# Latent attention: content and rotary rows of a head in one tile of 96 rows, one score product a head

## What is computed

```python
qc = (rmsnorm(cq, g_q) @ w_uq).reshape(B, T, C_HEADS, C_NOPE + C_ROPE)     # 4 heads, 64 + 32
q_nope, q_pe = qc[..., :C_NOPE], rope(qc[..., C_NOPE:], pos)
q_lat = jnp.einsum('bthn,hrn->bthr', q_nope, w_uk)
ckv = rmsnorm(ckv_raw, g_kv)
kpe = rope(kpe_raw[:, :, None, :], pos)[:, :, 0, :]                          # one for all heads
# mla_attend, for blocks of 128 queries over all keys before them:
s = (jnp.einsum('...qhr,...kr->...hqk', q_lat, ckv)
     + jnp.einsum('...qhp,...kp->...hqk', q_pe, kpe)) * ((C_NOPE + C_ROPE) ** -0.5)
p = jax.nn.softmax(s, axis=-1)
```

## Time and profile before

| | |
|---|---|
| Runs | 2032.88, 2032.96, 2033.73 us |
| Profiled execution | 2033.12 us; its span in the trace is 2031.3 us |
| TensorE busy | 2013.7 us, 99% of the span |
| VectorE, ScalarE, GpSimd busy | 82%, 48%, 18% |
| Share of TensorE in the chain that ended last | 94% |
| Mixing, layer 0 and layer 1 | about 405 to 619 us and 1401 to 1617 us |

### The profile page before, as it was taken

The page is one execution under the profiler, slowest core; times in us unless marked ns, Lnnn a source line. Parts: engine busy times, 40 slices in busy tenths (PEclk is TensorE's granted clock), DMA queues, the critical chain, the costliest instruction groups (busy, mean ns, idle before and its releaser), DMA issues.

```text
span 2031.3 us, 40732 instructions
## 1 busy us (share of the span) xinstructions
PE 2013.7 (99%) x15315; PEld 1961.2 (97%) x15315; DVE 1665.6 (82%) x2456; ACT 972.5 (48%) x1768; POOL 356.6 (18%) x218
## 2 busy tenths in 40 slices
PE   8999999999999999999999999999999999999998
PEld 7999999999889999999999999999987899999998
DVE  7999998755667999998689999976466599999975
ACT  6544453354546544453364444534546474444532
POOL 1222200042112222200012221002321213222000
PEclk8999999999999999999999999999999999999999
DMA  4323223342122232332222322324221123322321
GB/s 135 104 83 103 91 85 95 83 106 67 35 55 84 87 100 89 97 93 79 79 91 96 103 83 89 106 79 114 81 62 45 61 65 104 96 89 80 107 87 66
DMA packets 234855, 175.40 MB, mean 86 GB/s; under 512 B 35185, under 2 KB 231025, under 8 KB 234737
## 3 DMA queue, kind: packets, MB, share of 16 engines
q1 hardware_dynamic: 232624, 171.68, 28.3%
q10 hardware_dynamic: 2112, 2.10, 0.3%
HBM read 170.14 MB, written 3.62 MB: 86 GB/s over the span
## 4 chain that ended last, share of the span: by engine, by line
PE 94%; DVE 3%; ACT 2%; issue 1%; DMA 1%; ACTq 0%; DVEq 0%; SPq 0%
PE pair L1474 43%; PE pair L1423 32%; PE pair L1597 9%; PE pair L1530 2%; PE pair L1744 1%; PE pair L1724 1%; DVE t_parts L2067 1%; PE pair L1735 1%; PE pair L1730 1%; PE pair L1767 1%; PE pair L1752 1%; DMA x_tok<-in_x_prompt_dram 0%; ACT square L928 0%; PE pair L1760 0%; DVE t_parts L2350 0%
## 5 line engine op out<-in xcount | busy, mean ns | idle before, releaser
L1474 PE MATMUL pair<-t_parts,chunk_high 128*128 128x288 f32 x4480 | 893.5, 296 | 1.6 <-issue 1.2
L1474 PEld LDWEIGHTS pair<-t_parts,chunk_high 128*128 128x128 f32 x4480 | 719.5, 189 | 2.7 <-DVE chunk_low L2032 2.7
L1474 PE MATMUL pair<-t_parts,chunk_low 128*128 128x288 f32 x2240 | 661.6, 295 | 0.0
L1474 PEld LDWEIGHTS pair<-t_parts,chunk_low 128*128 128x128 f32 x2240 | 421.5, 188 | 0.0
L973 ACT ACTIVATE chunk_high<-chunk_sum 128x512 fp32r<-128x512 f32 x320 | 199.4, 631 | 380.4 <-DVE chunk_sum L2020 184.7
L870 POOL TENSOR_TENSOR chunk_low<-set_raw,chunk_high 128x512 fp32r<-128x512 f32 x160 | 229.4, 1443 | 716.4 <-ACT chunk_high L973 716.4
L864 POOL TENSOR_TENSOR w_low<-raw,w_high 128x1024 fp32r<-128x1024 f32 (+1 forms) x46 | 114.0, 2482 | 589.4 <-ACT w_high L921 589.4
L2032 DVE TENSOR_TENSOR chunk_low<-chunk_sum,chunk_high 128x512 fp32r<-128x512 f32 x320 | 207.1, 689 | 8.1 <-ACT chunk_high L973 0.5
L1423 PE MATMUL pair<-hidden_high,w_high 128*128 128x288 f32 x896 | 192.2, 296 | 0.0
L1423 PE MATMUL pair<-hidden_high,w_low 128*128 128x288 f32 x896 | 191.9, 296 | 0.0
L1423 PE MATMUL pair<-hidden_low,w_high 128*128 128x288 f32 x896 | 191.7, 296 | 0.0
(11 more groups left out here) (297 smaller groups left out, 3785.5 us busy)
## 6 DMA issues: line engine op xcount, KB each, us to landing
set_raw<-in_w_up_dram SPq DMA_DIRECT2D x44, 1024.0 KB, 5.4
set_raw<-in_w_gate_dram SPq DMA_DIRECT2D x44, 1024.0 KB, 5.4
raw<-in_w_down_dram SPq DMA_DIRECT2D x64, 448.0 KB, 3.6
down_raw<-in_w_down_dram SPq DMA_DIRECT2D x16, 1024.0 KB, 5.1
raw<-in_w_in_dram SPq DMA_DIRECT2D x20, 512.0 KB, 3.9
raw<-in_w_in_dram SPq DMA_DIRECT2D x16, 256.0 KB, 3.9
raw<-in_w_out_dram SPq DMA_DIRECT2D x8, 512.0 KB, 3.4
raw<-in_w_out_dram SPq DMA_DIRECT2D x16, 256.0 KB, 3.8
```

Source lines behind the costliest of these rows:

```text
L1474: mm = nc.tensor.matmul(out, c[:, j, p, :], tr[p // 2][:, seat(p), x, t, :], start=p == 0 and n == 0, stop=p == KP - 1 and n == 2)
```

## The change

Content and rotary rows of a head come to lie under each other in one tile of 96 rows: `keysT{h}` (64 content rows, 32 rotary rows, 832 keys) and `queriesT{h}` (576 columns), one pair of tiles a head. An MS unit is then one product of 96 rows a head, two a head in the sample unit (over the cache and over the new keys). The new keys stand ahead of the cache in the 832 columns.

To fill these tiles:

- `kn`: two ScalarE copies of 64 rows in place of one of 128, and behind those of `kn:0` three more that bring the rotated key to the heads 1 to 3 (32 rows, 576 columns, behind a wait on `rot:kpe.2`).
- `A:1` gets four ScalarE copies, in the list ahead of `T:8`: the rotated queries of each head to its tile (32 rows, 576 columns, behind a wait on `rot:qp.2`).
- `rot:kpe` gets four ScalarE copies, ahead of `E:9`: the cache's rotary key to each head (32 rows, 256 columns).
- `qn`: two VectorE copies of 64 rows in place of one of 128.
- `rot:qp` and `rot:kpe` multiply by the cosine in place, and so VectorE waits for TensorE's product by `rot32` ahead of its first instruction in place of its second.
- `tkpe` transposes from rows 64 to 95. `rot32` and `kpe_tok` lie elsewhere; the DMA of `rot32` is issued where it was.
- MS now waits for the last of the ScalarE copies of `kn:0`; the pair of `kn` is freed by its second copy.

```diff
@@ -215,9 +215,13 @@
     n = {"z": 0, "sumx": 1, "sumkv": 2, "sumq": 4, "tw": 1, "tv": 2, "tc": 2, "tk": 2, "tva": 2,
-         "rkv": 2, "tkpe": 2, "sw": 4, "rep": 1, "a": 1, "kn": 1, "E": 5, "O": 1, "ME": 2, "MO": 1, "ex": 1}.get(kind, 0)
+         "rkv": 2, "tkpe": 2, "sw": 4, "rep": 1, "a": 1, "kn": 2, "E": 5, "O": 1, "ME": 2, "MO": 1, "ex": 1}.get(kind, 0)
...
         n = 1 + arg
+    if step == "kn:0":
+        n = 2 + C_HEADS - 1
+    if step in ("A:1", "rot:kpe"):
+        n = C_HEADS
@@ -232,7 +236,7 @@
     kind, arg = split(step)
-    n = {"z": 1, "sumx": 2, "sumq": 3, "tckv": 2, "tw": 1, "rot": 3, "a": 4, "qp": 1, "qn": 1,
+    n = {"z": 1, "sumx": 2, "sumq": 3, "tckv": 2, "tw": 1, "rot": 3, "a": 4, "qp": 1, "qn": 2,
@@ -294,8 +298,12 @@
         return [("vector", f"rot:{arg}.0")]
-    if kind in ("z", "qp", "qn", "O", "MO", "A", "B"):
+    if kind in ("z", "qp", "O", "MO", "A", "B"):
         return [("vector", f"{step}.0")]
+    if kind == "qn":
+        return [("vector", f"{step}.1")]
+    if kind == "kn":
+        return [("scalar", f"{step}.1")]
@@ -335,7 +343,7 @@
         "S": lambda: ["tc.1"] if swa_unit(arg)[0] == 4 else [],
-        "MS": lambda: [f"kn:{mla_unit(arg)[1]}.0", "tc.1"],
+        "MS": lambda: [scalar_ops(s)[-1] for s in ("kn:0", "kn:1", "A:1", "rot:kpe")],
@@ -355,7 +363,7 @@
         "S": lambda: ["rot:k.2"] + [f"rot:q{2 * swa_unit(arg)[1] + e}.2" for e in range(2)],
-        "MS": lambda: ["rot:qp.2", "rot:kpe.2", f"qn:{mla_unit(arg)[1]}.0"],
+        "MS": lambda: ["rot:kpe.2", f"qn:{mla_unit(arg)[1]}.1"],
@@ -518,17 +526,16 @@
         KEYS = PAST + NT
-        knT = [mix(f"k_nopeT{j}", [P, KEYS]) for j in range(2)]
-        qnT = [mix(f"q_nopeT{j}", [P, NT]) for j in range(2)]
-        qpT = mix("q_peT", [P, NT])
-        kpeT = mix("kpeT", [P, NT])
+        kS = [mix(f"keysT{j}", [P, KEYS]) for j in range(C_HEADS)]
+        qS = [mix(f"queriesT{j}", [P, NT]) for j in range(C_HEADS)]
         kpe_rep = mix("kpe_rep", [P, NT])
-        rot32 = mix("rot32", [P, P])
...
         vc_tok = mix("vc_tok", [P, 7, C_HEADS * C_V])
-        kpe_tok = mix("kpe_tok", [P, 5, C_ROPE])
         assert cursor[0] <= temp0
+        rot32 = at("rot32", [P, P], F32, temp0 + U)
+        kpe_tok = at("kpe_tok", [P, 5, C_ROPE], F32, temp0 + U + P * 4)
+        NOPE, ROPE, BOTH = slice(0, C_NOPE), slice(C_NOPE, C_NOPE + C_ROPE), slice(0, C_NOPE + C_ROPE)
@@ -1265,6 +1272,15 @@
                         continue
+                    if step == "A:1":
+                        dve_did(act, layer, "rot:qp.2")
+                        for h_ in range(C_HEADS):
+                            copy(qS[h_][ROPE], zs[1][32 * h_:32 * h_ + 32], f"{step}.{h_}")
+                        continue
+                    if step == "rot:kpe":
+                        for h_ in range(C_HEADS):
+                            copy(kS[h_][ROPE, NT:KEYS], ckpeT[ROPE], f"{step}.{h_}")
+                        continue
@@ -1341,7 +1357,12 @@
                     elif kind == "kn":
-                        copy(knT[arg][:, :], flat(p)[:, 0:KEYS], f"{step}.0")
+                        for j in range(2):
+                            copy(kS[2 * arg + j][NOPE], flat(p)[64 * j:64 * j + 64, 0:KEYS], f"{step}.{j}")
+                        if arg == 0:
+                            dve_did(act, layer, "rot:kpe.2")
+                            for h_ in range(1, C_HEADS):
+                                copy(kS[h_][ROPE, 0:NT], kS[0][ROPE, 0:NT], f"{step}.{1 + h_}")
@@ -1688,11 +1709,12 @@
                         rows = C_ROPE if kind == "tkpe" else P
-                        src = {"tv": vT, "tckv": ckvT, "tkpe": kpeT, "tva": zs[1 - arg] if kind == "tva" else None}[kind]
+                        part = ROPE if kind == "tkpe" else slice(0, P)
+                        src = {"tv": vT, "tckv": ckvT, "tkpe": kS[0], "tva": zs[1 - arg] if kind == "tva" else None}[kind]
...
                             dst = ps[p][0:n, 0, t * rows:(t + 1) * rows] if t < 4 else ps[p][0:n, 1, 0:rows]
-                            mm = nc.tensor.transpose(dst, src[0:rows, t0:t0 + n], ident[0:rows, 0:rows])
+                            mm = nc.tensor.transpose(dst, src[part, t0:t0 + n], ident[part, part])
@@ -1711,7 +1733,7 @@
                         up = wuk[:, 2 * arg:2 * arg + 2, :].rearrange("p h n -> p (h n)")
-                        for col, keys, n in ((0, ckvT[:, 0:SEQ], SEQ), (SEQ, cT[:, P:3 * P], PAST), (SEQ + PAST, ckvT[:, SEQ:NT], DEC)):
+                        for col, keys, n in ((0, ckvT[:, 0:SEQ], SEQ), (SEQ, ckvT[:, SEQ:NT], DEC), (NT, cT[:, P:3 * P], PAST)):
@@ -1726,14 +1748,9 @@
                         for j in range(2):
-                            r = slice(64 * j, 64 * j + 64)
-                            nc.tensor.matmul(ps[p][0:nq, j, 0:W], qnT[pair][r, t0:t0 + nq], knT[pair][r, SEQ:KEYS] if i == 4 else knT[pair][r, 0:W],
-                                             start=True, stop=False)
-                        for k_pe, at0, col, n in ((ckpeT, 0, 0, PAST), (kpeT, SEQ, PAST, DEC)) if i == 4 else ((kpeT, 0, 0, W),):
-                            for j in range(2):
-                                r = slice(32 * (2 * pair + j), 32 * (2 * pair + j) + 32)
-                                mm = nc.tensor.matmul(ps[p][0:nq, j, col:col + n], qpT[r, t0:t0 + nq], k_pe[r, at0:at0 + n],
-                                                      start=False, stop=col + n == W)
+                            h_ = 2 * pair + j
+                            for col, at0, n in ((0, NT, PAST), (PAST, SEQ, DEC)) if i == 4 else ((0, 0, W),):
+                                mm = nc.tensor.matmul(ps[p][0:nq, j, col:col + n], qS[h_][BOTH, t0:t0 + nq], kS[h_][BOTH, at0:at0 + n], start=True, stop=True)
@@ -2451,7 +2468,7 @@
                     elif kind == "rot":
-                        dst = {"k": kT, "q0": qT[0], "q1": qT[1], "q2": qT[2], "q3": qT[3], "kpe": kpeT, "qp": qpT}[arg]
+                        dst = {"k": kT, "q0": qT[0], "q1": qT[1], "q2": qT[2], "q3": qT[3]}.get(arg)
@@ -2470,11 +2487,12 @@
                             dve.wait_ge(mix_in, layer * N_MIX_IN + N_MIX_IN)
-                        emit(nc.vector.tensor_tensor(dst[:, :], src[:, :], cos[:, :], ALU.mult), names[0])
                         pe_did(dve, layer, step)
+                        emit(nc.vector.tensor_tensor(src[:, :], src[:, :], cos[:, :], ALU.mult), names[0])
...
                         own(names[1])
-                        emit(nc.vector.tensor_tensor(dst[:, :], dst[:, :], work[:, :], ALU.add), names[2])
+                        out, part = (kS[0][ROPE, 0:NT], ROPE) if arg == "kpe" else (src[:, :], slice(0, P))
+                        emit(nc.vector.tensor_tensor(out, src[part], work[part], ALU.add), names[2])
@@ -2489,7 +2507,8 @@
                     elif kind == "qn":
-                        emit(nc.vector.tensor_copy(rows2(qnT[arg]), halves(p)), names[0])
+                        for j in range(2):
+                            emit(nc.vector.tensor_copy(rows2(qS[2 * arg + j])[NOPE], halves(p)[64 * j:64 * j + 64]), names[j])
```

## The result

The changed kernel takes 2042.9 us (median of 5 runs, 2041.71 to 2043.37) against 2033.1 for the kernel before (5 runs, 2032.88 to 2034.56): a ratio of 1.0045, 95% interval [1.0033, 1.0056]. It is 9.8 us slower. Forecast were 2037.2 and a range up to 2041.2, so the sign is right, and the size is more than twice what was expected. The profiled execution of the changed kernel took 2042.9 us, its span 2041.0.

What follows compares the result with a forecast made beforehand. TensorE, busy 99% of the span, was taken to bound the kernel. A layer: -3.1 (products) + 4.2 (ScalarE) + 1.0 (VectorE) = +2.1, two layers +4.2, so the median becomes 2037.2 us; range 2033.6 to 2041.2.

Steps and rivals of the forecast that it cites:

- rival 1, the clock: TensorE's clock halves for 3.4 us behind the waits at O:8, O:7, T:9: 1.7 us a layer, 2040.6; chance 0.13.
- only gaps of 0.09 us: TensorE in the old mixing hardly waits: gaps of 0.09 us only, where the part of the array in use changes.
- ScalarE ahead of MS:0: Added copies from kn:1 to vc:1 take 7.75 us and start T:9 4.2 us later a layer, between 3.0 and 5.3.
- the room: ScalarE's idle and overlap time before T:9, able to absorb 3.5 us of the added copies.
- The rival of cheap copies: 32-row copies on ScalarE cost a quarter: 4.0 us added work, a layer gains 1.6, 2029.8; chance 0.12.
- The products: MS score products on TensorE lose changes of the array's part: 3.1 us saved a layer, 2.8 to 3.3.
- MS:0's 0.25: Saving at score unit 0, which follows 64-row transposes whose kind the content product shared: 0.25 us.
- MT:7's 0.1: MT:7 loses perhaps 0.1 us a layer, since MS:8 covers less of ME:7.
- Unit 3: MS:3 stands between whole-array steps, loses three changes of the array's part, and saves 0.59 us.
- The rival of a 96-row part of its own: 96 rows keep 0.2 us at nine borders a layer: MS gives 1.3 instead of 3.1, 2040.8; chance 0.09.
- VectorE: Split qn copies delay T:6 by 0.3 and MS:1 by 0.6; with MT:7, 1.0 us lost a layer, 0.6 to 1.3.
- MS:1's 0.6: MS:1 on TensorE waits for qn:1's second VectorE copy and comes 0.6 us late.

Runs made afterwards that it cites:

- runs 8 and 9: Changed kernel with matmuls nobody reads filling only the wait at T:9 (8: 2041.5 us) or only the one at O:8 (9: 2041.9 us).
- experiment 3: Changed kernel with the eleven short 32-row copies on GpSimd in place of ScalarE: 2030.5 us, ratio 0.9984 to the kernel before.
- experiment 5: Kernel before, only qn taken out of PSUM by VectorE in two copies of 64 rows in place of one of 128: 2034.8 us against 2033.87.
- experiment 2: Changed kernel with matmuls nobody reads filling all three waits, at O:8, O:7 and T:9: 2039.1 us, ratio 1.0025 to the kernel before.
- run 10: Changed kernel with matmuls nobody reads in the waits at O:7 and T:9, only the one at O:8 left idle: 2039.5 us.
- experiment 7: Kernel of experiment 6 with qn:0's second copy also moved from VectorE to ScalarE, behind E:6's exponentials: 2034.9 us, ratio 1.0004 to the kernel before.
- experiment 6: Kernel of experiment 3 with qn:1's second copy of 64 rows moved from VectorE to ScalarE: 2028.6 us, ratio 0.9974 to the kernel before.

## Why the prediction missed

**The step that failed is the dismissal of rival 1, the clock.** The mechanism was named. It got a chance of 0.13, with the reason that the waits are in three pieces with products between. That reason doesn't hold: runs 8 and 9 show that two of the pieces are enough. The fall near the end that the prediction cites the earlier trace rows followed a stretch that was broken as well; its timeline of PE in the kernel before has one wait of 1.25 us, with products on both sides:

```profile
2020.41 1.26 PE L1838 MATMUL pair<-mean_d,sq_sum 128*128 128x1 f32 x10 [1.25 <-DVE sq_sum L1867]
```

The row spoke for the rival, and the text read it the other way. The prediction also said that only gaps of 0.09 us stand in the mixing of before; two waits of 0.55 and 0.74 us stand there too (ahead of 496.0 and 521.1), and the clock stayed at 1.00 behind them. In experiment 3 the largest single wait of a mixing is 0.77 us, and the clock stayed as well.

The price of the rival looks right, 1.7 us a layer against 1.6 and 2.0 measured net, but that is luck. It was half of one stretch of 3.4 us. The stretch was 6.8 us long; its first 1.2 us fell into T:9's wait and cost nothing, the rest cost 2.4 us in the first layer, and the hidden wait at MS:1 took 0.8 of these off again.

**ScalarE ahead of MS:0: right in kind, 0.35 short.** The added work is 7.8 us where 7.75 was summed, from the changed kernel's timeline of ACT, by starts:

```profile
544.63 1.75 ACT L1250 ACTIVATE keysT<-pair 64x832 f32<-64x832 f32 x2
546.40 2.79 ACT L1250 ACTIVATE queriesT<-z 32x576 f32<-32x576 f32 x4
549.22 0.65 ACT L1250 ACTIVATE probsT<-pair 128x256 f32<-128x256 f32 x2
549.89 1.32 ACT L1250 ACTIVATE keysT<-cache_kpeT 32x256 f32<-32x256 f32 x4
551.24 0.21 ACT L1306 ACTIVATE sink_exp<-sink_arg 64x4 f32<-64x4 f32 x1
...
552.94 1.74 ACT L1250 ACTIVATE keysT<-pair 64x832 f32<-64x832 f32 x2
554.70 1.82 ACT L1250 ACTIVATE keysT<-keysT 32x576 f32<-32x576 f32 x3
556.55 0.86 ACT L1250 ACTIVATE vc_tok<-pair 128x512 f32<-128x512 f32 x2
```

The queries' copies cost 2.82, the cache's 1.35, the key's 1.85, the second copies of kn 0.9 each. ScalarE is without idle time here, as forecast. T:9 is 4.55 later in place of 4.2, so the room was 3.3 and not 3.5. The rival of cheap copies is refuted: 32 rows cost 0.60 to 0.70 over 576 columns.

**The products: right.** -2.61 behind MS:1 where -2.75 stood (3.1 less MS:0's 0.25 and MT:7's 0.1). Unit 3 gave 0.59, to the hundredth. The rival of a 96-row part of its own is refuted: no gap stands at 573.02. The Trainium skill's "TensorEngine Tiling (Array Packing)", Available Configurations, lists row tilings of 128, 64 and 32 rows only, so that 96 rows are left to the whole array; the trace agrees, by this missing gap.

**VectorE: right, and partly hidden.** T:6 lost 0.42 where 0.3 was forecast: VectorE's two copies take 1.54, and E:6 then started after them with nothing saved. MS:1's 0.6 was a delay of 0.50 with the old products (experiment 5), and a wait of 0.77 and 0.63 in the two layers with the new (experiment 2). In the changed kernel it is not to be seen, since the slow clock covers it.

**The sum, put right.** Without the clock a layer has 0.42 + 4.55 + (7.13 - 6.58) - 2.61 = 2.9, so 2033.1 + 5.8 = 2038.9, where the kernel with the waits filled has 2039.1. With the clock, 1.6 and 2.0 more, 2042.5; the changed kernel has 2042.9. The error of 5.7 us is thus 3.6 of clock, 1.6 of terms that were each 0.1 to 0.4 short, and 0.5 that the parts outside the mixing differ by in the profile. The range failed because it took the terms' bounds for the likeliest case and then let the clock's 2040.6 sit inside, without adding the clock to the upper bound of the terms.

## What to carry to other kernels

Where a change makes the busiest engine wait, price the wait twice: once as idle time, and once as what the array's clock does behind it; here two waits of 0.7 to 1.7 us with products between them were enough to lower it. If the trace of before shows one fall of the clock, read what stood ahead of it, and add its price to the upper bound. And choose the engine for added copies by who waits behind it, not by how fast it copies: on GpSimd each copy took longer than on ScalarE, and the kernel became 12 us faster, though the copies there slowed some of VectorE's operations.

## What the hardware showed that I had not expected

- Idle time in pieces lowered the clock. Pieces of 1.5 and 0.7 us with some products between them did it in both layers (run 8), a single one of 1.5 in one of two layers (run 10).
- At the low clock a dependent engine catches up: the wait at MS:1 vanished in the changed kernel and was 0.77 us as soon as the clock was kept.
- One VectorE operation of 4 columns stood 2.21 us beside a rounding on GpSimd (experiment 7), and one 0.61 beside GpSimd's copies (experiment 3). In experiment 6 it began 0.7 us before the rounding and took 0.16, in experiment 7 0.2 us after it: a shift of 0.9 us between the two lists was enough to meet this.
